# Feed-forward matmuls that stream their columns from the last token to the first

## The reference

```
def conv_glu_ffn(x, w_up, conv_w, conv_b, w_down):
    h = causal_depthwise_conv(x @ w_up, conv_w, conv_b)
    gate, val = jnp.split(h, 2, axis=-1)
    return (jax.nn.silu(gate) * val) @ w_down

# in first_block, for each of the two layers, after the mixer
h = h + conv_glu_ffn(rmsnorm(h, ffn_norm[layer]), ffn_up[layer], ...)
```

## Time and profile before

| | |
|---|---|
| median of 3 runs | 2966.46 us (2966.22 to 2968.91) |
| profiled execution, span from first to last instruction | 2965.5 us |
| the same execution, time around the span | not shown by the page; the median stands 0.96 us above the span |
| TensorE matmuls, busy | 2901.6 us (98%), 15438 instructions |
| TensorE weight loads, busy | 2393.2 us (81%) |
| VectorE, busy | 1477.4 us (50%) |
| ScalarE, busy | 1163.9 us (39%) |
| mean granted TensorE clock | 0.997 of full speed |
| moved from and to HBM | 254.8 MB, mean 86 GB/s |

### The profile page before, as it was taken

How to read it: one execution, slowest core, us unless ns; L and a number is a source line. 1 busy time by engine, 2 the same in 40 slices (tenths; PEclk the granted TensorE clock), 3 DMA queues, 4 the chain that set the end, 5 groups by cost and what they waited for, 6 DMA issues and landing times.

```text
span 2965.5 us, 38348 instructions
## 1 busy us (share of the span) xinstructions
PE 2901.6 (98%) x15438; PEld 2393.2 (81%) x15438; DVE 1477.4 (50%) x2051; ACT 1163.9 (39%) x1856; POOL 146.0 (5%) x199
## 2 busy tenths in 40 slices
PE   9999999999999999999999999999999999999998
PEld 7778888776788887877888788868888788888776
DVE  5655455546463657366252543263455735453454
ACT  5444333526452344146233431173232743341452
POOL 1000000110000000100000300100001000200100
PEclk9999999999999999999999999999999999999999
DMA  5343332331332222210112221311113022321322
GB/s 185 122 158 105 113 128 85 129 130 38 136 107 98 99 87 76 82 54 22 60 43 76 85 68 57 101 60 64 57 64 101 21 82 78 108 91 66 121 75 85
DMA packets 48844, 260.98 MB, mean 88 GB/s; under 512 B 6872, under 2 KB 7904, under 8 KB 24896
## 3 DMA queue, kind: packets, MB, share of 16 engines
q1 hardware_dynamic: 36288, 213.75, 20.8%
q0 software_dynamic: 12416, 45.25, 4.5%
HBM read 250.50 MB, written 4.28 MB: 86 GB/s over the span
## 4 chain that ended last, share of the span: by engine, by line
PE 91%; DVE 4%; ACT 3%; DMA 1%; issue 1%; POOL 0%; SPq 0%; DVEq 0%; ACTq 0%
PE PS L897 15%; PE PS L898 15%; PE PS L899 15%; PE PS L874 7%; PE PS L876 7%; PE PS L875 7%; PE PS L833 3%; PE PS L835 3%; PE PS L834 3%; PE PS L1124 2%; PE PS L1086 1%; PE PS L1197 1%; PE PS L1179 1%; PE PS L1166 1%; PE PS L944 1%
## 5 line engine op out<-in xcount | busy, mean ns | idle before, releaser
L897 PE MATMUL PS<-HHX,WHX 128*128 128x512 f32 (+1 forms) x1440 | 504.6, 350 | 0.4 <-DVE WLX L2409 0.3
L898 PE MATMUL PS<-HL,WHX 128*128 128x512 f32 (+1 forms) x1440 | 503.4, 350 | 0.0
L1680 ACT ACTIVATE WHX<-W 128x2048 fp32r<-128x2048 f32 (+1 forms) x102 | 174.8, 1713 | 560.9 <-DMA W<-in_w 379.2
L899 PE MATMUL PS<-HHX,WLX 128*128 128x512 f32 (+1 forms) x1008 | 350.1, 347 | 0.0
L2409 DVE TENSOR_TENSOR WLX<-W,WHX 128x2048 fp32r<-128x2048 f32 x60 | 137.5, 2292 | 344.9 <-ACT WHX L1680 344.8
L897 PEld LDWEIGHTS PS<-HHX,WHX 128*128 128x128 f32 x1440 | 272.7, 189 | 38.3 <-DVE WLX L2409 1.5
L898 PEld LDWEIGHTS PS<-HL,WHX 128*128 128x128 f32 x1440 | 272.7, 189 | 34.9
L874 PE MATMUL PS<-HH,WH 128*128 128x512 f32 x672 | 261.7, 389 | 0.0
L876 PE MATMUL PS<-HH,WL 128*128 128x512 f32 x672 | 261.7, 389 | 0.0
L875 PE MATMUL PS<-HL,WH 128*128 128x512 f32 x672 | 261.6, 389 | 0.0
L2409 DVE TENSOR_TENSOR WL<-W,WH 128x2048 fp32r<-128x2048 f32 x68 | 155.7, 2290 | 177.8 <-ACT WH L1680 177.7
(11 more groups left out here) (553 smaller groups left out, 5813.8 us busy)
## 6 DMA issues: line engine op xcount, KB each, us to landing
W<-in_w SPq DMA_DIRECT2D x172, 1024.0 KB, 4.8
XC<-in_wm POOLq DMA_DIRECT2D x12, 1024.0 KB, 5.2
H<-in_wm POOLq DMA_DIRECT2D x12, 1024.0 KB, 6.0
W<-in_wb SPq DMA_DIRECT2D x24, 512.0 KB, 3.3
W<-in_w SPq DMA_DIRECT2D x8, 768.0 KB, 4.1
ARENA<-ARENA POOLq DMA_DIRECT2D x32, 128.0 KB, 2.3
ARENA<-mrow SPq DMA_DIRECT2D x12, 256.0 KB, 3.9
PR<-in_nbias POOLq DMA_DIRECT2D x12, 256.0 KB, 3.0
```

What stands on the lines that cost most here:

```text
L897: pe.matmul(dst, wh[:, s, c], hi[:, k, t0:t1], start=k == 0, stop=False)
L898: pe.matmul(dst, wh[:, s, c], lo[:, k, t0:t1], start=False, stop=False)
L899: mm = pe.matmul(dst, wl[:, s, c], hi[:, k, t0:t1], start=False, stop=k == kb - 1)
L1680: act.activation(dst[:, s, 0:n], W[:, s, 0:n], ACT.Copy).then_inc(wh_ready[s], 1)
```

## The change

The moving operand and the result of the three matmuls in `pe_split_unit` get a step of minus one along the tokens: column 511 is read and written first and column 0 last. Each output word is still the same sum. `pe_split_unit` is called by `pe_up` for all slabs but the first of a layer, and by `pe_down` for all but the first of a stage; nothing else calls it.

```
                     c = slice(k * SLAB + m * P, k * SLAB + m * P + P)
-                    pe.matmul(PS[:, b, :], WH[:, s, c], hi(k), start=k == 0, stop=False)
-                    pe.matmul(PS[:, b, :], WH[:, s, c], lo(k), start=False, stop=False)
-                    mm = pe.matmul(PS[:, b, :], WL[:, s, c], hi(k), start=False, stop=k == kb - 1)
+                    dst = PS[:, b, T - 1::-1]
+                    pe.matmul(dst, WH[:, s, c], hi(k)[:, T - 1::-1], start=k == 0, stop=False)
+                    pe.matmul(dst, WH[:, s, c], lo(k)[:, T - 1::-1], start=False, stop=False)
+                    mm = pe.matmul(dst, WL[:, s, c], hi(k)[:, T - 1::-1], start=False, stop=k == kb - 1)
                 mm.then_inc(slab_used[s] if m == 1 else full[b], 1)
```

## The result

The changed kernel takes 2985.77 us (median of 4 runs, 2982.66 to 2988.45) against 2967.47 us (4 runs): a ratio of 1.0062 with a 95% interval of 1.0048 to 1.0077. It is 18.3 us slower. The forecast of no change was wrong. The stated range, 2960 to 3575, holds the time, but only because it was drawn to reach half rate, which did not come. What came true is the second rival, a small price per matmul.

A forecast was written before the change was run, and what follows sets the result against it. TensorE's column streaming was taken to bound both feed-forward layers. The 2965.5 us span plus 0 for the reversal, with the median of runs 0.96 us above the span, gave 2966.5 us; range 2960 to 3575.

The forecast's parts named there:

- The forecast of no change: Whole kernel: reversing the reads and writes of 2808 matmuls costs nothing, 2966.5 us; chance 0.50, including the reversals being undone.
- half rate: Moving read or result write of all 2808 matmuls: going down, one word at a time; +602.5 us, 3569; chance 0.27.
- the second rival: Small price per changed matmul, at its start or line crossings: +37.6 us if doubled, or +120 us; chance 0.12.
- What bounds the kernel: Both feed-forward layers: TensorE's column streaming sets the end, so a nanosecond per matmul shows in full in the time.
- The count and the cost of a matmul: Up and down stages: 2808 changed matmuls at 0.2267 us from start to start fill 636.6 us of the span.
- I take zero: Changed matmuls: a backward walk touches the same words, neighbours following neighbours, as many times, so it adds 0 us.
- The two rows: Gapped keys at line 1166 (590 against 592 ns) and 129-column matmuls with odd-word writes (275 ns) showed no price.
- fixed part: Each changed matmul: 13.4 ns of its 226.7 ns that 512 columns at 0.417 ns each don't account for.
- the fourth: Rival for the changed matmuls: a gain, some of the fixed 13.4 ns goes, up to 37.6 us, 2929; chance 0.05.

## Why the prediction failed

**What bounds the kernel: right.** TensorE's column stream sets the end of both layers, nothing covers it, and 6.6 ns per matmul showed in full in the time: 18.5 us by the count, 18.6 in the two stretches, 18.3 between the medians.

**The count and the cost of a matmul: right.** 2808 matmuls at 226.7 ns; the product with 6.6 ns gives the loss.

**"I take zero": the failed step.** The two rows that I leaned on the earlier trace rows run at half the column rate, where a price could hide, as I wrote; I let them decide all the same. What misled was less the rate than the pattern: the halves swapped at full rate are free too (226.7 ns), and neither row descends. And I put against the second rival that no row shows a fixed part depending on addresses, and against the fourth that the fixed part has nothing to do with the order of the columns. Both are wrong: the fixed part is what moves. It is 13.3 ns when everything is in place and, at 512 columns, 20.0 when the moving read goes backward; it lay between 16 and 24 ns when the read started at column 16, 32 or 64 or ran from 511 to 16, or when the weights were fewer or read from other places. The rival's size, "doubled, 37.6 us", was twice what was measured: the part grew by 50%.

**Half rate: did not come.** I gave it 0.27, by the fast rate having a slower mode to fall into. The mode is there (453 ns at a step of two), but a step of minus one stays out of it. The Trainium skill's PSUM — Partial Sum Buffer (Specifications) says that any non-contiguous pattern slows matmuls significantly. Read by the letter, and with half rate as my own estimate of how much, it would have had the descending result cost 602 us; the result alone cost nothing (0.9990 to 1.0008), and the measurement decides.

**What is shown of the cause, and what isn't.** Shown: the price lies in the moving read and not in the result, belongs to each matmul, and is gone in groups of 64 words; and an untouched forward read gets the same 20 ns when only the weights' places change (all stages with every second column, 12 of 18 groups with the shift). So the excess depends on the moving read and on the weight read. That the two reads collide in the memory and lose turns is my reading of it, supported by the uneven starts with periods of four and six. One more sign for it: beside the moving read with a step of two, the loads of weights that lie in their old places are recorded as 207 ns (median) instead of 188:

```profile
912.59 0.21 PEld L883 LDWEIGHTS PS<-HIDH,WH 128*128 128x128 f32 x1 [0.24 <-issue]
```

No run shows a collision itself, and beside the backward read of the change the loads keep 188. The rule by which an excess of 13, 16, 18, 20 or 23 ns comes about stays open: shifting both reads alike did not restore 13.3, and the same places gave 16 in one stage and 20 in the next. Why going down from group to group costs 6.6 ns is open with it. A reversed weight read was not tried.

## What to carry to other kernels

A matmul at full rate has a part that isn't columns, here 13.3 of 226.7 ns, and it depends among other things on how the moving operand and the weights lie and in which direction the moving operand is read: read it from the distance of starts, and reckon with its moving by half when a tile's start, a step or the order changes, even where no instruction is added. Rows with other patterns don't price a pattern that none of them has. Where many matmuls have 256 columns, a backward read is worth a try; here it gave 0.16%.

## What the runs showed of the hardware that I had not expected

- A backward moving read of 512 columns costs 6.6 ns, one of 320 columns nothing (146.7 ns both ways), and one of 256 gains 1.6 ns.
- 496 columns forward from column 16 take as long as 512 from column 0 (226.7 ns): leaving out 16 tokens gained nothing.
- A moving read with a step of two runs at half rate (453 ns), a descending one nearly at full rate.
- Fewer weight columns made the stream slower: 230.0 ns with 64, 226.7 with 128.
- The same instructions on the same places settle at different distances in different stages: 202.8 and 206.7 ns for 448 columns from column 64.
- At 192 and at 128 columns, matmuls with a fresh weight load each both take about 111 ns.
